# Two modulation tiles at a visit, a longer stretch for them, and another order of the first loads

## The chip, the cores and the metric

One core of a Trainium2 chip runs the kernel. The metric is the time on the device in microseconds; the median of three runs is given. TensorE multiplies matrices (PE; its weight loads, PEld, overlap with it), VectorE is DVE, ScalarE is ACT, GpSimd is POOL, and SyncE (SP) issues nearly all transfers.

## What is computed

Two transformer blocks in a row on x (256 tokens by 1024), in fp32. The first block has a layer with differential attention beside an HGRN2 recurrence, and a layer with dilated attention, each with a feed-forward part and a gated embedding. The second block has two layers that mix gated linear attention, neighborhood attention and sliding-window attention, and it also carries a context of 256 tokens. Its norms are scaled, shifted and gated by modulations, which depend only on two small vectors `c` and `c_ctx`:

```python
s_lat = jax.nn.silu(c)
s_ctx = jax.nn.silu(c_ctx)
xc = ctx
for i in range(DEPTH):                       # DEPTH = 2
    mod = (s_lat @ w_mod[i] + b_mod[i])[:, None, :]
    mod_c = s_ctx @ w_mod[i] + b_mod[i]
    ...
    h = rms_norm_2(x, norm_mix[i]) * (1.0 + sc1) + sh1
    hc = rms_norm_2(xc, norm_mix[i]) * (1.0 + sc1c) + sh1c
    y, yc = token_mixers(h, hc, ...)
    x = x + g1 * y
```

## The kernel before

**Weights as a stream.** All weights stand in one array of tiles of 128 x 1024 fp32 (512 KB, eight blocks of 128 x 128). There are 410 tiles for the main path (x), read through a ring of 5 buffers (`ring`), and 96 modulation tiles (`w_mod`), read through `ring_mod` of 4 buffers. The context ("side" stream) reads 110 of the main path's later tiles a second time, through a ring of 2 (`ring_side`). For main and side tiles ScalarE makes a high part (`high`, L533) and VectorE the rest (`low`, L541), and each product of a block with 256 tokens is three matmuls, L566, L567 and L568 (L605 to L607 where tokens are stationary). So one such tile is 24 matmuls. x is split in the same way (L639, L647) before the first product.

**Modulations.** A modulation tile isn't split. Its products take two vectors at once: four matmuls (L695) on 32 columns of the array each, eight records of the profile. Eight tiles make a pass, after which ScalarE copies the rows (L723), TensorE turns them with `c_ident` (L707), and VectorE adds the bias (L737). There are 12 passes. `MOD_PLAN` spreads the tiles evenly over the first 250 us of the planner's clock. They depend on nothing in the first block, and the first block doesn't need them. The context's part depends on the last pass: `tensor_contexts` waits for it, and the loads of `ring_side` wait for the last tile to be used. `SIDE_PLAN` gives the pace of the context's tiles.

**The order of work** is made when the kernel is built. Each engine is a lane with a clock in microseconds, and each piece of work is a generator that says what it waits for (`yield name`) and how long it takes (`tick`). The planner takes the piece that can begin first; among those that can begin by then it takes the one of lowest rank, and of equal rank the one that was added first. A `Pace` has a low rank (first) while it is behind its plan, and a high one (only when nothing else is ready) when it is not. The result is a fixed order on every engine; a wrong guess of the planner becomes a wait on the chip, with all that is behind it on that engine. SP is such a lane too: `sync_loads`, `sync_tiles` and `sync_mod_tiles` are its pieces, and it issues in a fixed order.

**Start.** SP issues the two halves of x, the parameters (`par`), 11 constants, the context (`Xc`, 1 MB), five ring tiles and four modulation tiles, in this order. Parameters and constants count on one semaphore, `s_start`; whoever needs the parameters waits for the last constant. A load's time is planned as 0.1 us of SP, 1.3 us of distance to the next of the same piece, and 3.3 us to landing.

Of the kernel before, what the change touches and what calls it, by code (L numbers as in the profile page):

```python
# [103 lines left out]
TB = 8  # L104
RING, SPLIT = 5, 3
RING_SIDE, SPLIT_SIDE = 2, 2
RING_MOD = 4
MAIN_TILES, MOD_TILES = 410, 96
# [5 lines left out]
GLOBAL_CONSTS = ["ident", "meanD", "mean128", "mean64", "before", "after", "cols"]  # L114
ROPE_CONSTS = ["cos1", "sin1", "rot1"]
# [130 lines left out]
def T_us(n, passes=1):  # L246
    return max(n * passes / 2270.0, 0.06) + 0.006


def A_us(n):  # L250
    return 0.2 + n / 1200.0


def V_us(n):
    return 0.15 + n / 960.0
# [6 lines left out]
class Program:  # L262
    def __init__(self, nc, ctx, io):
# [19 lines left out]
        self.s_pool = signal("gpsimd_steps")  # L283
        self.s_raw_mod = [signal(f"mod_tile_loaded{i}") for i in range(RING_MOD)]
        self.s_xload = [signal(f"x_loaded{i}") for i in range(2)]
        self.s_start, self.s_ctx = signal("constants_loaded"), signal("ctx_loaded")
        self.s_consts, self.s_bias = signal("stage_constants_loaded"), [signal(f"bias_loaded{i}") for i in range(2)]
        self.s_p, self.s_wa2, self.s_out = signal("p_loaded"), signal("wa2_loaded"), signal("stored")

        self.main = Stream(self, "main", RING, SPLIT, None)  # L290
        self.side = Stream(self, "side", RING_SIDE, SPLIT_SIDE, second_tiles("c", 0) + second_tiles("c", 1))
        self.s_tile, self.s_low, self.split = [], self.main.s_low.sem, 0
        self.mod_blocks, self.blocks, self.loaded = [], [], None
        x, c = self.px, self.pc = Path("x", 1), Path("c", 0)
        x.stream, c.stream = self.main, self.side

# [15 lines left out]
        for w in (x, c):  # L312
# [11 lines left out]
            n = 512 if w is x else SEQ  # L324
# [152 lines left out]

def sync_loads(k):
    nc, io, D_, x = k.nc, k.io, k.D, k.px
    for i, half in enumerate((slice(0, DC // 2), slice(DC // 2, DC))):  # L480
        nc.sync.dma_start(x.X[:, half, :], io["x"][:, half]).then_inc(
            *D_.tick(k.s_xload[i], 0.1, ("x loaded", i), by=16, later=5.0))
    k.add(D_, sync_tiles(k, k.main), 0)
    yield None
    for buffer, name in [(k.par, "params")] + [(k.c[n], n) for n in GLOBAL_CONSTS + ROPE_CONSTS + ["causal"]]:
        nc.sync.dma_start(buffer[:, :], io[name]).then_inc(
            *D_.tick(k.s_start, 0.1, ("loaded", name), by=16, later=4.0))
        yield None
    k.marks["constants"] = D_.last
    k.add(D_, sync_mod_tiles(k), 1)  # L490
    nc.sync.dma_start(k.pc.X[:, :, :], io["ctx"]).then_inc(
        *D_.tick(k.s_ctx, 0.1, ("ctx loaded",), by=16, later=9.0))
    k.add(D_, sync_tiles(k, k.side), 1)


def sync_tiles(k, st):

    nc, D_ = k.nc, k.D
    n = MAIN_TILES if st.plan is None else len(st.plan)
    if st is k.side:  # L500

        D_.wait_for((yield "mod used", MOD_TILES - 1))
    for j in range(n):
        if j >= st.n_ring:
            D_.wait_for((yield st.name, "used", j - st.n_ring))
        else:
            yield None
        at = j if st.plan is None else TILE_AT[st.plan[j]]
        nc.sync.dma_start(st.ring[:, j % st.n_ring, :], k.io["stream"][at]).then_inc(
            *D_.tick(st.s_raw[j % st.n_ring], 0.1, (st.name, "raw", j), by=16, later=3.3))  # L510
        D_.clock += 1.3


def sync_mod_tiles(k):

    nc, D_ = k.nc, k.D
    for j in range(MOD_TILES):
        if j >= RING_MOD:
            D_.wait_for((yield "mod used", j - RING_MOD))
        else:  # L520
            yield None
        nc.sync.dma_start(k.ring_mod[:, j % RING_MOD, :], k.io["stream"][MAIN_TILES + j]).then_inc(
            *D_.tick(k.s_raw_mod[j % RING_MOD], 0.1, ("mod raw", j), by=16, later=3.3))
        D_.clock += 1.3


def scalar_high(k, st):
# [125 lines left out]
def vector_setup(k):  # L653
    nc, V = k.nc, k.V
    nc.vector.memset(k.zeros[:, :], 0.0).then_inc(*V.tick(k.s_vec, V_us(SEQ)))
    nc.vector.memset(k.keep[:, :], 1.0).then_inc(*V.tick(k.s_vec, V_us(SEQ)))
    V.wait_ge(k.s_vec, V.last)
    nc.vector.memset(k.keep[:, :].rearrange("p (c t) -> p c t", t=CH)[:, :, 0:1], 0.0).then_inc(
        *V.tick(k.s_vec, 0.15, ("keep",)))
    nc.vector.memset(k.cs[:, :, :], 0.0).then_inc(*V.tick(k.s_vec_bg, V_us(256), ("cs", "zero")))  # L660
    V.wait_ge(k.s_start, (yield "constants"))
    nc.vector.tensor_scalar(k.negsink, k.col("sink", 0, 12), -1.0, None, ALU.mult).then_inc(
        *V.tick(k.s_vec, 0.15, ("negsink",)))


def scalar_setup(k):
    nc, A = k.nc, k.A
    A.wait_ge(k.s_start, (yield "constants"))
    cc = k.col("cc", 0, 16)
    A.wait_ge(k.s_vec_bg, (yield "cs", "zero"))  # L670
    k.tables("silu")
    nc.scalar.activation(k.cs[:, :, 0:2], cc.rearrange("p (c s) -> p c s", s=2), ACT.Silu).then_inc(
        *A.tick(k.s_act_bg, 1.5, ("cs",)))
# [8 lines left out]
def tensor_modulations(k):  # L682
    nc, T = k.nc, k.T
    T.wait_ge(k.s_act_bg, (yield "cs",))
    for layer in range(DEPTH):
        for i in range(MOD_PASSES):
            b = yield from k.pc.gemm.take(T, ("row", layer, i))
            k.bank_of["rows", layer, i] = b
            for c in range(DC):
                tile = len(k.mod_blocks) // TB  # L690
                k.mod_blocks += [("w_mod_2", layer, c, 8 * i + j) for j in range(8)]
                raw = k.ring_mod[:, tile % RING_MOD, :]
                T.wait_ge(k.s_raw_mod[tile % RING_MOD], (yield "mod raw", tile))
                for j in range(4):
                    m = nc.tensor.matmul(k.bank[b][32 * j:32 * j + 32, 0:256], k.cs[:, c, :],  # L695
                                         raw[:, 256 * j:256 * j + 256], start=(c == 0), stop=(c == DC - 1),
                                         skip_group_check=True)
                if c == DC - 1:
                    m.then_inc(*T.tick(k.s_mod_rows, MOD_US, ("rows", layer, i), ("mod used", tile)))
                else:  # L700
                    m.then_inc(*T.tick(k.s_used_mod, MOD_US, ("mod used", tile)))
                yield None
            T.wait_ge(k.s_act_bg, (yield "row", layer, i))
            b = yield from k.pc.gemm.take(T, ("mod", layer, i))
            k.bank_of["mod turned", layer, i] = b
            for j in range(2):
                m = nc.tensor.transpose(k.bank[b][:, j * P:(j + 1) * P], k.rows[:, j * P:(j + 1) * P],  # L707
                                        k.c["ident"][:, :])
            m.then_inc(*T.tick(k.s_mod_turned, 2 * T_us(256), ("mod turned", layer, i)))
            yield None  # L710


MOD_US = 0.5


def scalar_modulations(k):
# [24 lines left out]
def rstd(k, mean, out, eps, read, key):  # L741

    nc, A = k.nc, k.A
    n = out.shape[1]
    k.tables("ln")
    nc.scalar.activation(out, mean, ACT.Ln, bias=k.c["cols"][:, eps:eps + 1]).then_inc(
        *A.tick(k.s_rstd, A_us(n), read))
    A.wait_ge(k.s_rstd, A.last)
    k.tables("exp")
    nc.scalar.activation(out, out, ACT.Exp, scale=-0.5).then_inc(*A.tick(k.s_rstd, A_us(n), key))  # L750
    yield None
# [398 lines left out]
def tensor_squares(k, w, tag):  # L1150
    nc, T, n = k.nc, k.T, SEQ
    yield tag, "square", 0
    b = yield from w.banks.take(T, (tag, "log"))
    k.bank_of[tag, "squares"] = b
    for i in range(DC):
        T.wait_ge(k.s_squares, (yield tag, "square", i))
        nc.tensor.matmul(k.bank[b][:, 0:n], k.c["meanD"][:, :], w.SQ[:, k.sq_of[tag, i], 0:n], start=(i == 0),
                         stop=(i == DC - 1)).then_inc(*T.tick(k.s_sums, T_us(n, 4), (tag, "summed", i)))
        yield None
# [274 lines left out]
def vector_lambda(k):  # L1434
    nc, V = k.nc, k.V
    c = k.px.small[:, 48:56]
    lp = k.col("lam", 0, 256)
    V.wait_ge(k.s_start, (yield "constants"))
    for i in range(2):
        a, b = lp[:, 128 * i:128 * i + 64], lp[:, 128 * i + 64:128 * i + 128]  # L1440
        nc.vector.tensor_tensor_reduce(a, a, b, 1.0, 0.0, ALU.mult, ALU.add, c[:, i:i + 1]).then_inc(
# [906 lines left out]
def load_stream(k, tiles):  # L2348
    assert tiles >= MAIN_TILES + MOD_TILES
    k.add(k.D, sync_loads(k), 0)  # L2350
# [26 lines left out]
        return self.late if self.done() < due else self.rank  # L2377


MOD_PLAN = [(0, 0), (250, MOD_TILES)]  # L2380
SIDE_PLAN = [(250, 0), (820, 35), (1400, 110)]


def emit(k):
# [3 lines left out]
    k.add(T, tensor_products(k, x), 1)  # L2388
    mods = Pace(k, lambda: len(k.mod_blocks) / TB, MOD_PLAN, -3, 3)
    side = Pace(k, lambda: len(k.side.blocks) / TB, SIDE_PLAN, -6, 5)  # L2390
    k.add(T, tensor_modulations(k), mods)
# [5 lines left out]
    k.add(A, x_high(k), 0)  # L2397
    k.add(V, x_low(k), 0)
    k.add(V, vector_setup(k), 1)
    k.add(A, scalar_setup(k), mods)  # L2400
    k.add(A, scalar_modulations(k), mods)
    k.add(V, vector_modulations(k), mods)
# [318 lines left out]
```

## Time and profile before

| | |
|---|---|
| runs | 1936.05, 1930.65, 1936.8 us (median 1936.05) |
| the profiled execution's own time | 1936.03 us |
| its span | 1934.7 us |
| mean granted clock of TensorE | 0.979 of full speed |
| busy | PE 1830.1 us (95%), DVE 1268.5 (66%), ACT 1000.2 (52%) |
| HBM read | 331.55 MB, 172 GB/s over the span |

All positions in time are microseconds from the span's start. Rows of matmuls show the modelled duration, which overlaps with the next one; the distance from start to start is what a matmul costs. "Idle before" is the time in which the engine had nothing under way, with what ended it.

### The profile page before, as it was taken

How to read it: one execution, taken by the hardware profiler on the slowest of the kernel's cores; microseconds unless marked ns; L12 is line 12 of the kernel's file. 1: busy time of each engine (PE TensorE's matmuls, PEld its weight loads, DVE VectorE, ACT ScalarE, POOL GpSimd, SP SyncE). 2: the span in 40 equal slices, each digit the busy share in tenths (PEclk: the TensorE clock that was granted, in tenths of full speed). 3: DMA queues.
4: the chain of work that ended last, by engine and by line, in shares of the span. 5: the costliest groups of instructions: out<-in, count | busy, mean ns of one | idle time of the engine just before them, and what ended most of it. 6: DMA issues, size and time to landing. Idle time of an engine off the chain costs nothing. (4 is left out here: it accounts for less than half of the span.)

```text
span 1934.7 us, 35649 instructions
## 1 busy us (share of the span) xinstructions
PE 1830.1 (95%) x14792; PEld 1675.2 (87%) x14792; DVE 1268.5 (66%) x2327; ACT 1000.2 (52%) x1748; POOL 77.5 (4%) x78
## 2 busy tenths in 40 slices
PE   5998899999999989999988999999999989889997
PEld 3775699998888969999988998899999978589997
DVE  3535565667867786666666677776775667756665
ACT  3444443547755565454465565554554455544443
POOL 0000100002000020000020010100100000100000
PEclk9999999999999999999998999999999989989999
DMA  8898875563454425555544444355555533235553
GB/s 320 296 314 296 266 235 188 181 202 113 138 171 131 141 66 166 190 182 190 184 131 156 152 153 132 110 164 185 179 172 172 176 120 110 66 104 181 185 185 120
DMA packets 93824, 334.91 MB, mean 173 GB/s; under 512 B 10960, under 2 KB 12880, under 8 KB 93536
## 3 DMA queue, kind: packets, MB, share of 16 engines
q1 hardware_dynamic: 92016, 327.33, 51.6%
q0 software_dynamic: 1648, 5.31, 0.9%
q8 instruction: 117, 1.92, 0.4%
q14 instruction: 43, 0.35, 0.1%
HBM read 331.55 MB, written 1.05 MB: 172 GB/s over the span
## 5 line engine op out<-in xcount | busy, mean ns | idle before, releaser
L541 DVE TENSOR_TENSOR low<-ring,high 128x1024 fp32r<-128x1024 f32 x410 | 501.5, 1224 | 260.4 <-ACT high L533 257.6
L566 PE MATMUL bank<-XHx,high 128*128 128x256 f32 x2096 | 613.1, 293 | 36.3 <-DVE XLx L647 20.9
L533 ACT CAST high<-ring 128x1024 fp32r<-128x1024 f32 x410 | 428.6, 1045 | 329.9 <-PE bank L568 277.4
L567 PE MATMUL bank<-XLx,high 128*128 128x256 f32 x2096 | 594.9, 284 | 0.0
L568 PE MATMUL bank<-XHx,low 128*128 128x256 f32 x2096 | 594.6, 284 | 0.0
L566 PEld LDWEIGHTS bank<-XHx,high 128*128 128x128 f32 x2096 | 401.8, 192 | 67.5 <-issue 47.1
L567 PEld LDWEIGHTS bank<-XLx,high 128*128 128x128 f32 x2096 | 403.0, 192 | 1.0
L568 PEld LDWEIGHTS bank<-XHx,low 128*128 128x128 f32 x2096 | 403.1, 192 | 0.0
L566 PE MATMUL bank<-XHc,high_side 128*128 128x256 f32 x608 | 181.7, 299 | 13.3 <-DVE low_side L541 11.7
L567 PE MATMUL bank<-XLc,high_side 128*128 128x256 f32 x608 | 172.8, 284 | 0.0
L568 PE MATMUL bank<-XHc,low_side 128*128 128x256 f32 x608 | 172.4, 284 | 0.0
L541 DVE TENSOR_TENSOR low_side<-ring_side,high_side 128x1024 fp32r<-128x1024 f32 x110 | 136.6, 1243 | 51.8 <-ACT high_side L533 49.7
L533 ACT CAST high_side<-ring_side 128x1024 fp32r<-128x1024 f32 x110 | 115.2, 1047 | 73.9 <-DMA ring_side<-in_stream 73.5
L566 PE MATMUL bank<-hidden_high,high 128*128 128x256 f32 x512 | 143.5, 280 | 0.0
L568 PE MATMUL bank<-hidden_high,low 128*128 128x256 f32 x512 | 143.4, 280 | 0.0
L567 PE MATMUL bank<-hidden_low,high 128*128 128x256 f32 x512 | 142.6, 279 | 0.0
L566 PEld LDWEIGHTS bank<-XHc,high_side 128*128 128x128 f32 x608 | 116.7, 192 | 24.4 <-issue 15.5
L567 PEld LDWEIGHTS bank<-XLc,high_side 128*128 128x128 f32 x608 | 116.9, 192 | 0.3
L568 PEld LDWEIGHTS bank<-XHc,low_side 128*128 128x128 f32 x608 | 117.1, 193 | 0.0
L566 PE MATMUL bank<-x_hidden_high,high 128*128 128x256 f32 x352 | 99.4, 282 | 1.8 <-DVE x_hidden_low L1281 1.8
L567 PE MATMUL bank<-x_hidden_low,high 128*128 128x256 f32 x352 | 98.4, 279 | 0.0
L568 PE MATMUL bank<-x_hidden_high,low 128*128 128x256 f32 x352 | 98.1, 279 | 0.0
(448 smaller groups left out, 3078.9 us busy)
## 6 DMA issues: line engine op xcount, KB each, us to landing
ring<-in_stream SPq DMA_DIRECT2D x410, 512.0 KB, 3.6
ring_side<-in_stream SPq DMA_DIRECT2D x110, 512.0 KB, 3.7
ring_mod<-in_stream SPq DMA_DIRECT2D x96, 512.0 KB, 5.4
x_nb<-in_rpb POOLq DMA_DIRECT2D x6, 256.0 KB, 3.3
x_late_NB<-in_rpb POOLq DMA_DIRECT2D x6, 256.0 KB, 3.2
Xx<-in_x SPq DMA_DIRECT2D x2, 512.0 KB, 4.6
Xc<-in_ctx SPq DMA_DIRECT2D x1, 1024.0 KB, 6.5
out<-y SPq DMA_DIRECT2D x8, 128.0 KB, 2.0
```

The lines of the kernel that those rows point to most:

```text
L533: nc.scalar.copy(st.high[:, j % st.n_split, :], st.ring[:, j % st.n_ring, :]).then_inc(*A.tick(st.s_high, A_us(TB * P), (st.name, "high", j)))
L541: nc.vector.tensor_tensor(st.low[:, j % st.n_ring, :], st.ring[:, j % st.n_ring, :], st.high[:, j % st.n_split, :].bitcast(F32), ALU.subtr ...
L566: nc.tensor.matmul(out, wh, xh, start=(i == 0), stop=False)
L567: nc.tensor.matmul(out, wh, xl, start=False, stop=False)
L568: m = nc.tensor.matmul(out, wl, xh, start=False, stop=(c == ks[-1]))
```

## The change

- `sync_loads` issues half of x, a ring tile, the parameters, the other half of x and a second ring tile; then the constants, then the context. The tiles' piece and the modulations' piece are added before the constants, at ranks 0 and 1, but behind `sync_loads` in the lane.
- The parameters get a semaphore of their own (`s_par`). `negsink`, the lambda and the silu of `c` wait for it alone. The turns of the modulations, the root of the norms and the sums of squares wait for the constants instead.
- A load's planned time: 0.45 us of SP, and `landing` keeps one account for all loads that use it: each takes 1.5 us behind the one before, and 2.0 us on top.
- `tensor_modulations` takes two tiles at a visit (`MOD_BATCH`), without a step between them, and both must have landed in the plan. The planned time of a tile is 0.43 us, and 0.45 us for the visit.
- `MOD_PLAN` ends at 480 rather than 250. `SIDE_PLAN` begins at 480 rather than 250 and has 35 tiles at 850 rather than 820; its end stays.

```diff
 def sync_loads(k):
     nc, io, D_, x = k.nc, k.io, k.D, k.px
+    tiles = sync_tiles(k, k.main)
+    next(tiles)
     for i, half in enumerate((slice(0, DC // 2), slice(DC // 2, DC))):
+
         nc.sync.dma_start(x.X[:, half, :], io["x"][:, half]).then_inc(
-            *D_.tick(k.s_xload[i], 0.1, ("x loaded", i), by=16, later=5.0))
-    k.add(D_, sync_tiles(k, k.main), 0)
+            *D_.tick(k.s_xload[i], 0.45, ("x loaded", i), by=16, later=landing(k, D_)))
+        next(tiles)
+        if i == 0:
+            nc.sync.dma_start(k.par[:, :], io["params"]).then_inc(
+                *D_.tick(k.s_par, 0.45, ("params",), by=16, later=landing(k, D_)))
+    k.add(D_, tiles, 0)
+    k.add(D_, sync_mod_tiles(k), 1)
     yield None
-    for buffer, name in [(k.par, "params")] + [(k.c[n], n) for n in GLOBAL_CONSTS + ROPE_CONSTS + ["causal"]]:
-        nc.sync.dma_start(buffer[:, :], io[name]).then_inc(
-            *D_.tick(k.s_start, 0.1, ("loaded", name), by=16, later=4.0))
+    names = GLOBAL_CONSTS + ROPE_CONSTS + ["causal"]
+    for name in names:
+        nc.sync.dma_start(k.c[name][:, :], io[name]).then_inc(*D_.tick(k.s_start, 0.45, by=16, later=4.0))
         yield None
+
+    for name in names:
+        k.marks["loaded", name] = D_.last
     k.marks["constants"] = D_.last
-    k.add(D_, sync_mod_tiles(k), 1)
...
+def landing(k, lane):
+
+    k.loads = max(k.loads, lane.clock) + 1.5
+    return k.loads - lane.clock + 2.0
...
         nc.sync.dma_start(st.ring[:, j % st.n_ring, :], k.io["stream"][at]).then_inc(
-            *D_.tick(st.s_raw[j % st.n_ring], 0.1, (st.name, "raw", j), by=16, later=3.3))
-        D_.clock += 1.3
+            *D_.tick(st.s_raw[j % st.n_ring], 0.45, (st.name, "raw", j), by=16, later=landing(k, D_)))
...
         for i in range(MOD_PASSES):
+            first = len(k.mod_blocks) // TB
+            yield "mod raw", first + MOD_BATCH - 1
             b = yield from k.pc.gemm.take(T, ("row", layer, i))
             k.bank_of["rows", layer, i] = b
             for c in range(DC):
                 tile = len(k.mod_blocks) // TB
+                if c % MOD_BATCH == 0:
+
+                    yield "mod raw", tile + MOD_BATCH - 1
                 k.mod_blocks += [("w_mod_2", layer, c, 8 * i + j) for j in range(8)]
                 raw = k.ring_mod[:, tile % RING_MOD, :]
-                T.wait_ge(k.s_raw_mod[tile % RING_MOD], (yield "mod raw", tile))
+                T.wait_ge(k.s_raw_mod[tile % RING_MOD], k.marks["mod raw", tile])
...
-                yield None
+                if c % MOD_BATCH == 0:
+                    T.spend(0.45)
+            yield None
             T.wait_ge(k.s_act_bg, (yield "row", layer, i))
             b = yield from k.pc.gemm.take(T, ("mod", layer, i))
             k.bank_of["mod turned", layer, i] = b
+            T.wait_ge(k.s_start, (yield "constants"))
...
-MOD_US = 0.5
+MOD_US, MOD_BATCH = 0.43, 2
...
-MOD_PLAN = [(0, 0), (250, MOD_TILES)]
-SIDE_PLAN = [(250, 0), (820, 35), (1400, 110)]
+MOD_PLAN = [(0, 0), (480, MOD_TILES)]
+SIDE_PLAN = [(480, 0), (850, 35), (1400, 110)]
```

## Rows read from the trace of the kernel before

**Rows 1.** Busy time by stretch: length, busy (instructions) PE PEld DVE ACT POOL, clock, DMA.

```profile
21.00:140.00 119.00, 117.94 (x987) 88.65 (x988) 54.67 (x130) 52.54 (x106) 0.00 (x0) 1.00 0.88 304
140.00:245.00 105.00, 92.90 (x779) 62.61 (x777) 59.52 (x114) 47.30 (x81) 9.55 (x10) 0.93 0.84 285
245.00:420.00 175.00, 175.00 (x1486) 171.15 (x1484) 104.78 (x144) 81.23 (x124) 0.53 (x1) 1.00 0.61 197
420.00:480.00 60.00, 53.76 (x394) 49.08 (x393) 46.15 (x85) 42.17 (x81) 10.26 (x8) 0.91 0.43 143
```

**Rows 2.** Groups up to 500 us: busy us, mean ns, idle before, its releaser.

```profile
L695 PE MATMUL bank<-ring_mod,TMPc 128*32 128x256 f32 x768 | 61.7, 409 | 9.1 <-DMA ring_mod<-in_stream 9.1
```

**Rows 3.** The start in order of time: start us, us, engine, line, operation.

```profile
0.74 0.86 SPq L481 DMA_DIRECT2D Xx<-in_x  x2
...
8.35 3.04 SPq L509 DMA_DIRECT2D ring<-in_stream  x5
...
15.68 1.04 ACT L533 CAST high<-ring 128x1024 fp32r<-128x1024 f32 x1 [13.66 <-DMA ring<-in_stream]
...
16.76 1.23 DVE L541 TENSOR_TENSOR low<-ring,high 128x1024 fp32r<-128x1024 f32 x1 [4.14 <-ACT high L533]
...
20.93 0.55 PE L566 MATMUL bank<-XHx,high 128*128 128x256 f32 x1 [20.93 <-DVE XLx L647]
...
21.28 0.41 PE L567 MATMUL bank<-XLx,high 128*128 128x256 f32 x1
...
21.49 0.41 PE L568 MATMUL bank<-XHx,low 128*128 128x256 f32 x1
```

**Rows 4.** Transfers, 0 to 21 us in 40 slices, and issues with us to landing.

```profile
GB/s 0 0 0 148 304 289 195 265 406 390 318 397 356 321 313 291 248 294 355 417 449 328 437 375 359 437 414 414 437 398 429 421 406 429 414 414 437 398 390 445
...
ring<-in_stream SPq DMA_DIRECT2D x5, 512.0 KB, 8.9
...
Xx<-in_x SPq DMA_DIRECT2D x2, 512.0 KB, 4.6
```

**Rows 5.** Timeline of TensorE around a visit of one tile and of two.

```profile
65.39 0.28 PE L567 MATMUL bank<-XLx,high 128*128 128x256 f32 x1
65.51 0.28 PE L568 MATMUL bank<-XHx,low 128*128 128x256 f32 x1
65.72 0.64 PE L695 MATMUL bank<-ring_mod,TMPc 128*32 128x256 f32 x8
66.29 0.38 PE L566 MATMUL bank<-XHx,high 128*128 128x256 f32 x1
...
243.03 1.07 PE L695 MATMUL bank<-ring_mod,TMPc 128*32 128x256 f32 x16
244.03 0.39 PE L566 MATMUL bank<-XHx,high 128*128 128x256 f32 x1
```

**Rows 6.** Timeline of TensorE from the last modulation tile to the context's first product.

```profile
428.01 0.64 PE L695 MATMUL bank<-ring_mod,TMPc 128*32 128x256 f32 x8
...
435.27 1.22 PE L1157 MATMUL bank<-SQx,c_meanD 128*128 128x256 f32 x2 [2.96 <-ACT SQx L1167]
...
438.22 0.41 PE L567 MATMUL bank<-p_low,high 128*128 128x256 f32 x1
...
442.05 0.47 PE L566 MATMUL bank<-XHc,high_side 128*128 128x256 f32 x1
```

**Rows 7.** Modulation matmuls alone, by stretch: PE busy (x), PEld busy (x), clock, DMA.

```profile
21.00:140.00 119.00, 28.58 (x360) 7.44 (x360) 1.00 0.88 304
140.00:245.00 105.00, 27.98 (x344) 8.38 (x344) 0.93 0.84 285
245.00:420.00 175.00, 4.47 (x56) 1.10 (x56) 1.00 0.61 197
```

**Rows 8.** Waits of TensorE from 140 to 245 us: us, times, longest.

```profile
PE bank L695 <- DMA ring_mod<-in_stream: 8.1, 6, 2.2
```

**Rows 9.** Instructions with the context's high parts: PE, PEld, DVE, ACT busy.

```profile
420.00:480.00 60.00, 21.12 (x102) 16.84 (x103) 8.55 (x7) 7.78 (x8) 0.91 0.43 143
```

More of the change, by code:

```diff
@@ L285, in __init__ @@
         self.s_xload = [signal(f"x_loaded{i}") for i in range(2)]
-        self.s_start, self.s_ctx = signal("constants_loaded"), signal("ctx_loaded")
+        self.s_par, self.s_start, self.s_ctx = signal("params_loaded"), signal("constants_loaded"), signal("ctx_loaded")
         self.s_consts, self.s_bias = signal("stage_constants_loaded"), [signal(f"bias_loaded{i}") for i in range(2)]
@@ L292, in __init__ @@
         self.s_tile, self.s_low, self.split = [], self.main.s_low.sem, 0
-        self.mod_blocks, self.blocks, self.loaded = [], [], None
+        self.mod_blocks, self.blocks, self.loaded, self.loads = [], [], None, 0.0
         x, c = self.px, self.pc = Path("x", 1), Path("c", 0)
@@ L522, in sync_mod_tiles @@
         nc.sync.dma_start(k.ring_mod[:, j % RING_MOD, :], k.io["stream"][MAIN_TILES + j]).then_inc(
-            *D_.tick(k.s_raw_mod[j % RING_MOD], 0.1, ("mod raw", j), by=16, later=3.3))
-        D_.clock += 1.3
+            *D_.tick(k.s_raw_mod[j % RING_MOD], 0.45, ("mod raw", j), by=16, later=landing(k, D_)))
 def scalar_high(k, st):
@@ L660, in vector_setup @@
     nc.vector.memset(k.cs[:, :, :], 0.0).then_inc(*V.tick(k.s_vec_bg, V_us(256), ("cs", "zero")))
-    V.wait_ge(k.s_start, (yield "constants"))
+    V.wait_ge(k.s_par, (yield "params",))
     nc.vector.tensor_scalar(k.negsink, k.col("sink", 0, 12), -1.0, None, ALU.mult).then_inc(
@@ L667, in scalar_setup @@
     nc, A = k.nc, k.A
-    A.wait_ge(k.s_start, (yield "constants"))
+    A.wait_ge(k.s_par, (yield "params",))
     cc = k.col("cc", 0, 16)
@@ L744, in rstd @@
     n = out.shape[1]
+    A.wait_ge(k.s_start, (yield "constants"))
     k.tables("ln")
@@ L1152, in tensor_squares @@
     yield tag, "square", 0
+    T.wait_ge(k.s_start, (yield "constants"))
     b = yield from w.banks.take(T, (tag, "log"))
@@ L1437, in vector_lambda @@
     lp = k.col("lam", 0, 256)
-    V.wait_ge(k.s_start, (yield "constants"))
+    V.wait_ge(k.s_par, (yield "params",))
     for i in range(2):
```

## The prediction

> **What bounds the kernel now.** I first read the stretches [rows 1]: for each stretch they give how long TensorE was busy, its granted clock and the DMA share. From 21 to 140 us TensorE is busy 117.94 of 119 us, and from 245 to 420 us all of 175. There every microsecond of TensorE work is a microsecond of the kernel. It is idle before 21 us, for 12.1 us in 140 to 245 and for 6.2 in 420 to 480. In these two later stretches the granted clock falls under 1.00 (0.93, 0.91), so part of the work runs at 1.2 GHz. The rest of the span holds no edit, only work that is ordered anew. So the time is TensorE's work, plus its idle time, plus what the lower clock costs, and the sum below is made of changes in these three.
>
> Then I read the groups of instructions up to 500 us [rows 2]: before modulation matmuls TensorE stands idle for 9.1 us, all of it until a tile has landed. Next the start in order of time [rows 3]: x is issued at 0.74 us, then parameters, eleven constants and the context, and the first ring tile only from 8.35. Its cast starts at 15.68, and the first matmul at 20.93. [Rows 4] say how long transfers took and at what rate.
>
> **First loads.** After the change SP issues half of x, tile 0, the parameters, the other half of x and tile 1, and only then the eleven constants, the context and the other tiles: the constants are a planner part that comes before the ring's tiles at each step, so tile 2 still stands behind all of them. Tile 0 takes the place of the second half of x, issued near 1.2 us; with the 4.6 us of x [rows 4] it lands near 6, its high part takes 1.04 and its low part 1.23 us [rows 3], and with the splitting of x the first matmul comes near 8.5. Tile 1 ends the first 2.6 MB (two halves of x, two tiles, parameters, and 0.26 MB that GpSimd loads), which the slices of [rows 4], 0.525 us each, give by about 10 us, so it is landed by 11 and ready by 13.3. Tile 2 has the same bytes ahead of it as today and lands when it does today, issued near 9.3 and landed 8.9 us later [rows 4]: 18.2, ready at 20.5. A tile is 24 matmuls; at full clock they start 0.12 us apart [rows 5], so 2.85 us, and at the low clock 0.21 us apart [rows 3], so 5 us. Tile 0 ends near 13.5, tile 1 near 16.3, and TensorE then waits 4.2 us for tile 2. The start therefore gives two tiles, 5.7 us, and 0.4 us from 20.93 to 20.5: 6.1 us, not the 12.4 by which the first matmul is earlier. Bounds: 4 (tile 1 late too) and 9.
>
> The low clock enters here. After an idle time of 2.96 us at 432 to 435 [rows 6] the matmuls that follow take 0.41 us as those of the start do [rows 3], not the 0.28 of the full clock, so I count the restart at 20.5 as cold as today's start and take nothing for the clock. The Trainium skill, "TensorE: Matmul & The Clock Gate", section "HAM oscillation", warns of just this, short work followed by a wait for a load, and this speaks against starting early: by that rule the early tiles run cold and the restart too, which is what I counted. Without the restart being cold it would give about 2 us more.
>
> The Trainium skill, "DMA: Bandwidth & Descriptors", section "Specifications", names about 358 GB/s from HBM for a core; the slices from 12 us on in [rows 4] show 359 to 445, most of them over 400. By the page's figure the 1.6 MB of context and tile 2 would take 0.6 us longer than at 0.41 MB/us; the measurement decides.
>
> **Two tiles at a visit.** A single visit today [rows 5]: the last matmul before starts at 65.51, the visit at 65.72, the next product at 66.29; without it the next would start 0.12 later, so a visit costs 0.66 us. A double one without a stall starts at 243.03 and the next product at 244.03: 0.21 + 1.00 - 0.12 = 1.09 us. Pairing saves 0.23 us. Today's 96 tiles (768 records in [rows 2], eight a tile) are taken in 76 visits, counted as runs of this matmul with no other between, of which [rows 5] show two; after the change in 48: 28 x 0.23 = 6.4 us. Bounds 4 (a visit merged in an idle stretch is worth nothing) and 6.4.
>
> **Over twice the stretch.** By records [rows 7] hold 45 tiles in 21 to 140 us, 43 in 140 to 245, 7 in 245 to 420; the last one comes at 428.01 [rows 6]. The plan falls from 96/250 to 96/480 = 0.2 tiles per us, so about 24 tiles fall before the main path's first idle stretch. The others are not removed: they fill the idle places from there on, 16 or so are forced between the feed-forward products, and some 15 to 20 are left for the idle place after them. By itself this only moves work. What it can win is stalls: of the 9.1 us, 8.1 lie in 140 to 245, in six waits of up to 2.2 us [rows 8], in bursts for which the planner believes in a load each 1.4 us. The new `landing` says 1.5 us per load on one account for all streams and lets a visit wait for both tiles, so visits are put later. But the ring holds four tiles still, only two visits, and the main chain there (its scan, exponentials and LayerNorm) has waits of its own. I take 5 us, bounds 0 and 9.1. Queued behind such a wait are the products of that chain, on the same engine; that is why any of it counts.
>
> **Contexts later.** The context's loads wait until the last modulation tile is used. That one ran at 428.01 today, the context's first product followed at 442.05 [rows 6], and 21.12 us of context products (high part; in all 102 x 1.5 / 24 = 6.4 tiles, 18 us of issue) filled 420 to 480 [rows 9]. Afterwards 15 to 20 modulation tiles (0.55 us each, 8 to 11 us) fill this place first, and the context comes some 25 us later. These 18 us of context work are then forced in where TensorE is full, while the 8 to 11 us of modulations have left the full places: the idle time is what differs, 7 to 10 us, less what the main path gains because ScalarE and VectorE (46 of 60 us busy) do not split context tiles there. I take a loss of 4; bounds: a gain of 6.2 (all idle time there goes [rows 1]) and a loss of 21.1.
>
> The waits on the parameters alone (negsink, lambda, silu) and the new waits on constants cost nothing: the last of today's constants lands before 12.0 us, two tiles more ahead of them add under 3 us, and the first matmul that reads one comes after 30; if they were late, tile products behind it would wait.
>
> **Sum.** The profiled execution took 1936.03 us, span 1934.7, and the median of the three runs is 1936.05. 1936 - 6.1 - 6.4 - 5 + 4 = 1922.5 us.
>
> **Rivals.**
> - *Starved start, stalls stay.* Tile 1 late as well, everything cold: 1936 - 2 - 6.4 - 0 + 4 = 1931.6. For it: DMA share 0.9 over the whole start; against it: tile 1 has only 2.4 MB before its end.
> - *More than summed.* The stalls go (9.1) and the idle time of 420 to 480 too (6.2): 1936 - 6.1 - 6.4 - 9.1 - 6.2 = 1908.2. For it: VectorE is freed there. Against: today's context work is what fills it.
> - *Slower: the filler is missing.* Where the 21.1 us of context products stood, TensorE stands idle, and its clock falls as in this stretch today: 1936 - 6.1 - 6.4 - 5 + 21.1 = 1939.6. It decides once the idle time in this stretch grows by over 17.5 us. For it: little but modulations is ready there, at 0.55 us of work per 512 KB against 2.85; against: 15 tiles are left over, and the main path's own LayerNorm and gate take the engines.
> - *The pace does nothing* (modulations run ahead in idle places just as before) and only order changes: within 0.3%.
>
> **Chances.** Forecast 0.50, own range 1914 to 1930. More than summed 0.18, starved start 0.15, slower 0.13, nothing 0.04. The bound of 0.3% is 5.8 us, about what a measurement of this kernel can tell from no change: faster means under 1930.2. The forecast, the larger gain and a part of the starved start give faster 0.71; same 0.15; slower 0.14. For 8 in 10 the range takes in the starved start and most of the large gain: 1905 to 1936.
>
> **What the profile after would show.** First matmul near 8.5 us, then a wait of 4 us before the third tile; L695's rows sixteen at a time; waits for ring_mod under 5 us; PE full up to an earlier first idle stretch, some 20 us sooner; about 15 modulation tiles after the feed-forward part, and the first context product after 440 us of today's count; idle time there about 10 us. I am wrong if that idle time reaches 20 us, if tile 2 comes earlier than 15 us, or if new stalls stand behind 480 us, where every order of work is planned anew.

## The result and the profile after

The changed kernel takes 1897.3 us (median of 4 runs, 1895.24 to 1903.14) against 1935.53 for the kernel before (4 runs): a ratio of 0.9813, 95% interval 0.9801 to 0.9826, so 38.2 us faster. The forecast was 1922.5, a gain of 13.5, and the range ended at 1905. The direction is right and the size is not. The profiled execution is the slowest of its four: 1903.14 us, span 1901.8.

The stretches of [rows 1] after the change, in the same columns (length, busy and instructions of PE, PEld, DVE, ACT, POOL, then granted clock, DMA share, GB/s), then the rest of the span:

```profile
21.00:140.00 119.00, 117.31 (x916) 94.48 (x917) 67.83 (x146) 67.70 (x131) 0.00 (x0) 0.96 0.77 267
140.00:245.00 105.00, 96.20 (x844) 79.93 (x843) 64.16 (x117) 45.37 (x81) 10.09 (x10) 0.95 0.75 250
245.00:420.00 175.00, 173.18 (x1528) 161.29 (x1526) 99.62 (x142) 79.25 (x125) 2.89 (x3) 1.00 0.75 239
420.00:480.00 60.00, 58.86 (x428) 51.81 (x425) 48.95 (x86) 39.13 (x64) 7.02 (x7) 1.00 0.71 236
480.00:1480.00 1000.00, 974.37 (x7958) 918.73 (x7957) 703.08 (x1329) 554.40 (x991) 48.79 (x43) 1.00 0.50 156
```

The idle time of 420 to 480 fell from 6.2 us to 1.1 and the clock there rose from 0.91 to 1.00; in 140 to 245 idle fell from 12.1 to 8.8. From 21 to 140 us the clock is 0.96 where it was 1.00. The transfers are spread: their share fell before 245 us and rose after. The modulation matmuls alone, same stretches (PE, PEld):

```profile
21.00:140.00 119.00, 17.77 (x256) 6.94 (x256) 0.96 0.77 267
140.00:245.00 105.00, 17.07 (x224) 5.78 (x224) 0.95 0.75 250
245.00:420.00 175.00, 15.23 (x224) 5.64 (x224) 1.00 0.75 239
420.00:480.00 60.00, 4.25 (x68) 1.77 (x64) 1.00 0.71 236
```

That is 32, 28, 28 and 8 tiles where [rows 7] had 45, 43 and 7. Waits of TensorE up to 500 us (us, times, longest):

```profile
PE bank L580 <- DVE low L555: 10.9, 2, 9.0
PE bank L714 <- DMA ring_mod<-in_stream: 6.6, 9, 1.5
PE bank L1181 <- ACT SQx L1191: 3.4, 2, 2.8
PE bank L580 <- DVE XLx L661: 2.4, 1, 2.4
```

The start in order of time (start, duration, engine, line), against [rows 3]:

```profile
0.74 0.39 SPq L484 DMA_DIRECT2D Xx<-in_x  x1
...
1.18 0.42 SPq L525 DMA_DIRECT2D ring<-in_stream  x1
...
2.12 0.63 SPq L484 DMA_DIRECT2D Xx<-in_x  x1
...
2.79 0.56 SPq L525 DMA_DIRECT2D ring<-in_stream  x1
...
9.01 0.55 PE L580 MATMUL bank<-XHx,high 128*128 128x256 f32 x1 [9.01 <-DVE low L555]
...
9.58 1.66 SPq L525 DMA_DIRECT2D ring<-in_stream  x3
...
14.20 1.23 DVE L555 TENSOR_TENSOR low<-ring,high 128x1024 fp32r<-128x1024 f32 x1 [3.49 <-DMA c_causal<-in_causal]
...
15.48 0.41 PE L580 MATMUL bank<-XHx,high 128*128 128x256 f32 x1 [1.93 <-DVE low L555]
...
18.00 1.04 ACT L547 CAST high<-ring 128x1024 fp32r<-128x1024 f32 x1 [5.33 <-DMA ring<-in_stream]
...
18.95 0.70 ACT L653 CAST XHx<-Xx 128x256 fp32r<-128x256 f32 x2
...
20.69 0.58 PE L580 MATMUL bank<-XHx,high 128*128 128x256 f32 x1 [2.45 <-DVE XLx L661]
```

The first product is at 9.01 instead of 20.93. But TensorE then stops twice. The stop that ends at 15.48 is a wait for the second tile's low part. Its high part was done at 12.36, but VectorE made the low part only at 14.20, when the last constant (`c_causal`) had landed. The kernel gives the reason: the first statement of `vector_attention` is a wait for the constants, and the planner put it in VectorE's order just ahead of this low part. The kernel before has the same statement; there VectorE had nothing else to do at that time. The stop that ends at 20.69 is not a wait for the third tile: it is for the last two parts of x, which ScalarE cast at 18.95, behind the cast of the third tile, which had waited 5.33 us for its load.

In the waits above, 9.0 of the 10.9 us for `low` are the start and 1.9 the stop at 15.48.

Two views of a visit and of the end of the modulations, against [rows 5] and [rows 6]:

```profile
314.26 0.28 PE L582 MATMUL bank<-XHx,low 128*128 128x256 f32 x1
314.47 1.07 PE L714 MATMUL bank<-ring_mod,TMPc 128*32 128x256 f32 x16
315.47 0.39 PE L580 MATMUL bank<-XHx,high 128*128 128x256 f32 x1
...
447.25 1.93 PE L714 MATMUL bank<-ring_mod,TMPc 128*32 128x256 f32 x32
...
472.03 0.28 PE L580 MATMUL bank<-XHc,high_side 128*128 128x256 f32 x1
```

**Where the time went.** All orders run the same products, so I laid every TensorE start-to-start distance to one of these (us, from one trace each; products' own time is equal and left out; "low clock" is the excess over the full-clock distance):

| | before | after | plans alone (e1) |
|---|---|---|---|
| first product | 20.9 | 9.0 | 21.7 |
| modulation visits, with their waits | 77.6 | 65.2 | 74.5 |
| other small gaps, under 0.45 each | 149.1 | 143.0 | 143.9 |
| idle, from main tile 0 to 35 | 0.0 | 8.1 | 0.5 |
| idle, tiles 92 to 110 | 6.4 | 0.7 | 0.7 |
| idle, all other | 60.5 | 58.5 | 51.8 |
| low clock | 19.2 | 16.3 | 13.1 |
| sum of these | 333.7 | 300.8 | 306.2 |

Tiles 92 to 110 are the stretch between the first block's dense feed-forward products and the following layer's: 415.8 us onwards before, 389.3 to 471.8 after. The row of visits takes in every wait just before or after modulation matmuls, also those in tiles 92 to 110: the idle time there by the profile's own rows is 3.0 us in the changed kernel and 4.7 in e1, not 0.7. A profile is one execution, and one kernel's runs lie up to 16 us apart, partly with the clock. So I also use the mean over all runs of the span times (1 minus the granted clock), called *clock loss* below: it bounds what a full clock would give, and it is more than the clock costs, since TensorE is also idle or held by others in some of that time (in the profile before it is 40.6 us, and the table has 19.2). Before it is 35 us in each comparison (mean span about 1933, clock 0.982); after, 27.5 (1896.9, 0.9855). So at most some 7 of the 38 us are clock.

### The profile page after: what moved, and what is told of

It reads as the page before. It is cut to its first block and busy times, and to the rows that moved or that the text cites. A ratio compares the mean times of both kernels' runs of the same rounds, so it can differ in the third digit from the quotient of the medians.

```text
span 1901.8 us, 35689 instructions
## 1 busy us (share of the span) xinstructions
PE 1812.8 (95%) x14792; PEld 1673.5 (88%) x14792; DVE 1267.8 (67%) x2327; ACT 995.9 (52%) x1744; POOL 79.2 (4%) x78
## 5 line engine op out<-in xcount | busy, mean ns | idle before, releaser
L580 PE MATMUL bank<-XHx,high 128*128 128x256 f32 x2096 | 612.0, 292 | 21.2 <-DVE low L555 10.9
L580 PE MATMUL bank<-XHc,high_side 128*128 128x256 f32 x608 | 177.7, 292 | 7.8 <-DVE low_side L555 7.7
L580 PEld LDWEIGHTS bank<-hidden_high,high 128*128 128x128 f32 x512 | 96.2, 188 | 2.4 <-issue 2.4
```

The lines of the kernel that those rows point to most:

```text
L580: nc.tensor.matmul(out, wh, xh, start=(i == 0), stop=False)
```

## The experiments

All ratios are to the kernel before, run beside it, with 95% intervals. Because the planner finds no order for some paces, a few kernels use the nearest one that it finds; the diffs show them.

**e1 to e4: one part alone, or all but one.** e1 is the kernel before with only the paces:

```diff
-MOD_PLAN = [(0, 0), (250, MOD_TILES)]
-SIDE_PLAN = [(250, 0), (820, 35), (1400, 110)]
+MOD_PLAN = [(0, 0), (480, MOD_TILES)]
+SIDE_PLAN = [(480, 0), (840, 35), (1400, 110)]
```

> The kernel before with the two paces alone: modulations over 480 us, contexts from 480 (35 tiles at 840, since with 850 the planner finds no order for this kernel). Theory A (the paces carry the gain behind 420 us: context work leaves the stretch where the main path is held by ScalarE and VectorE, and lands in places that were idle): 12 to 20 us faster, about 1920, with idle time in 420 to 480 no larger than before and less idle in 640 to 1060. Theory B (the new load times of the planner carry it): within 4 us of before. Theory C (any new order moves the time by some us without a cause in the edit): anything between -8 and +8, with the gain spread over stages.

e2 is the kernel before with only the planned times of loads: 0.45 us of SP each, and `later=landing(k, D_)` for x and the tiles.

> The kernel before with the planner's new load times alone (0.45 us of SP, one account of 1.5 us a load, 2.0 us on top); order of the first loads, visits and paces as before. Theory A: the waits of modulation matmuls for their tiles fall from 9.1 to under 5 us, the rest stays: 2 to 6 us faster. Theory B: 12 us faster or more, with less idle time all over the span.

e3 is the kernel before with only the new order of the first loads and the semaphore `s_par`, planned by the old times.

> The kernel before with the order of the first loads and the separate semaphore of the parameters alone. Theory A: first matmul near 9 us, then waits; worth 3 to 6 us, since tile 2 and the late parts of x hold the products until about 20.7. Rival: the whole 11.9 us by which the first matmul is earlier.

e4 is the changed kernel with the old `MOD_PLAN` and `SIDE_PLAN`.

> The changed kernel with the two old paces (modulations over 250 us, contexts from 250 with 35 tiles at 820). Theory A: it loses the 12 to 20 us of the paces and keeps start, pairs and fewer stalls: 1912 to 1920. Theory B: it stays within 4 us of the changed kernel, 1897 to 1901.

| kernel | median us | ratio | clock loss us |
|---|---|---|---|
| e1 paces alone | 1908.14 | 0.9856 (0.9817 to 0.9895) | 23.8 |
| e2 load times alone | 1928.24 | 0.9963 (0.9945 to 0.9982) | 35.5 |
| e3 first loads alone | 1933.47 | 0.9984 (0.9962 to 1.0006) | 35.7 |
| e4 all but the paces | 1917.55 | 0.9917 (0.9885 to 0.9949) | 38.7 |

The paces, which I had booked as a loss of 4, gain 26 us alone and some 20 on top of the rest. The load times gain 7, but not in the way that I expected: TensorE's wait for modulation tiles stays at 8.9 us in e2, where it was 9.1. Where these 7 us come from isn't shown. The first loads alone give 3, inside their interval.

**e5 and e6: is it the place where the contexts begin?** The first theory was that the context's products, moved behind the norm and gate, stop being in the main path's way there. e5 holds the last modulation tile back until main tile 105 is used, with the modulations' pace as before:

```diff
+                if tile == MOD_TILES - 1:
+                    yield "main", "used", 105
...
-SIDE_PLAN = [(250, 0), (820, 35), (1400, 110)]
+SIDE_PLAN = [(440, 0), (845, 35), (1400, 110)]
```

> The kernel before, 95 modulation tiles as today; only the last one is held in the order until main tile 105 is used (in the changed kernel it comes there), so that the context's products begin there too, at a pace from 440 us with 35 tiles at 845. Theory A (it is the place at which the context begins, away from the norm and the gate between the two layers, that gives most of the 26 us of the two paces): 12 to 20 us faster than before. Rival D (it is the modulations spread over 480 us, which leave the first stretches and fill the later idle places): within 4 us of before, or slower, as TensorE has nothing to fill 430 to 470 with.

e6 changes the context's pace alone, to `[(480, 0), (835, 35), (1400, 110)]`.

> The kernel before with the contexts' pace alone (from 480 us, 35 tiles at 835): context products may still fill places near 440 us in which nothing else is ready, but are not forced. Theory A: less than half of the gain of the held tile, 0 to 8 us faster, since they still begin in the norm's stretch. Rival E (it is the forced context tiles that cost): 12 us faster or more.

Measured: e5 1935.52 us, 1.0004 (0.9987 to 1.0021); e6 1934.59 us, 0.9995 (0.9977 to 1.0013). In e5 the first context product moved from 442 to 489 us and won nothing. So the place alone isn't the cause.

**e7: the modulations' pace alone** (`MOD_PLAN` 480, the rest as before).

> The kernel before with the modulations' pace alone (480 us); contexts keep their plan (from 250, 35 tiles at 820), but can't begin before the last modulation tile. Theory A: the context begins late anyway and then is forced to catch up with its plan; most of the gain stays, 12 to 24 us faster. Rival E: little gain, since the tiles are forced in.

Measured: 1923.5 us, 0.9935 (0.9911 to 0.9959), clock loss 30.4: 12 of the 26 us.

**e9, e13, e14: other lengths of the pace** in the changed kernel: 380, 430 and 500 instead of 480. e12 is the changed kernel again, in the same comparison as e9.

> The changed kernel with the modulations' pace ending at 380 us rather than 480; contexts still from 480. The last modulation tiles then come before the norm between the two layers of the first block (near 400 us), and nothing is left to fill it: contexts are not due. Theory F (what the two paces win is that modulation tiles, cheap and free of ScalarE and VectorE, fill that norm's stretch, where before them context tiles or nothing did): idle and low clock there come back, 6 to 12 us slower than the changed kernel, 1903 to 1910. Rival G (only that modulations leave the first 140 us counts): under 3 us slower.

> The changed kernel once more, to stand beside these on the same chip: 1895 to 1900 us. Its profile should show the first matmul at 9.0 us again, the second start at 15.5, the third at 20.7; the low clock may lie differently from execution to execution.

> The changed kernel with the modulations spread over 430 us of the planner's clock instead of 480 (380 gave 1910.1, 480 gives 1899.2 and 1897.3). Theory of the filler (modulation tiles left for the stretch between the feed-forward part and the next layer's products replace idle time and low clock there): fewer tiles are left over than the 22 of 480 and more than the none of 380, so the time lies between, near 1903, and the idle time of that stretch between 0.7 and 6 us. Rival (380 was a bad order by chance, the pace itself is indifferent): as the changed kernel, within 3 us of 1898.

> The changed kernel with 500 instead of 480. Theory of the filler: the stretch is filled already with 22 tiles, idle only 0.7 us, so more tiles win nothing there: 1896 to 1902, the stretch up to the context's first product grows by the few tiles moved into it and the one before shrinks alike. A loss, over 1904, would show that the context, which waits for the last tile, becomes late.

| pace | median us | ratio | modulation tiles after main tile 92 | idle + low clock, tiles 92 to 110, without waits at visits | clock loss |
|---|---|---|---|---|---|
| 380 (e9) | 1910.11 | 0.9876 (0.9855 to 0.9897) | 0 | 8.6 | 35.9 |
| 430 (e13) | 1923.09 | 0.9935 (0.9911 to 0.9958) | 10 | 10.4 | 46.9 |
| 480 (e12) | 1899.19 | 0.9823 (0.9797 to 0.9849) | 20 | 0.7 | 28.1 |
| 500 (e14) | 1902.5 | 0.9833 (0.9809 to 0.9857) | 24 | 0.0 | 29.5 |

The windows of tiles 92 to 110, of e9, then of e13, then of the changed kernel:

```profile
395.00:480.20 85.20, 79.55 (x521) 72.64 (x520) 65.71 (x114) 55.88 (x100) 10.03 (x9) 0.96 0.48 151
```

```profile
395.70:482.70 87.00, 81.30 (x559) 70.94 (x558) 63.49 (x110) 51.93 (x92) 11.58 (x9) 0.94 0.59 188
```

```profile
389.30:471.80 82.50, 79.54 (x620) 66.50 (x619) 61.98 (x108) 52.15 (x92) 9.91 (x9) 1.00 0.79 264
```

The changed kernel does 99 more matmuls than e9 (160 of its 620 are modulations) in 2.7 us less. TensorE is idle in it for 3.0 us, against 5.7 in each of the others, and it has full clock where e9 and e13 have 0.96 and 0.94. Waits of e9's TensorE there show how (idle before it in brackets); the matmul after the longest takes 0.55 us, not 0.39:

```profile
411.49 0.39 PE L580 MATMUL bank<-p_high,high 128*128 128x256 f32 x1 [0.75 <-ACT e L1342]
...
413.39 1.17 PE L1181 MATMUL bank<-SQx,c_meanD 128*128 128x256 f32 x4 [0.92 <-ACT SQx L1191]
...
425.53 0.55 PE L580 MATMUL bank<-XHx,high 128*128 128x256 f32 x1 [3.36 <-DVE XLx L1219]
```

So in this stretch the tiles left over do act as filler, and it is no slope: 10 are used up before the waits come (the last one at main tile 97, at 418.1 us; the first wait over 0.9 us ends at 423.5) and save nothing; 20 reach to tile 106 and save about half of the idle time and all of the low clock. That is some 5 of the 11 us by which e9 is slower than e12; the rest lies in other stages. The time of the whole kernel follows the filler less well: my expectation for 430, a time between, missed by 20 us, and 430 is 11 to 13 us slower than 380, which has no filler at all. Of e13's 22 us over e12 in mean span, up to 19 are clock loss, and by the two traces the low clock cost it more than e12 in six of eight stages (30.7 us against 15.2 in all). Why this order is put at the low clock so often isn't settled.

**e8, e10, e15, e16: the start.** e8 puts two more ring tiles, four in all, ahead of the constants (two more `next(tiles)` before they are issued). e10 puts the first loads back in their old order in the changed kernel.

> The changed kernel with ring tiles 2 and 3 issued before the constants and the context (the planner believes in landings near 9 and 11 us; in truth tile 2 now lands near 13 rather than 17). Theory A (tile 2 behind 2 MB of constants and context, and the last two parts of x cast after it, hold the products until 20.7 us): the wait before 20.69 shrinks from 7 us to 2, the clock falls less; 3 to 6 us faster than the changed kernel, about 1892. Rival: no gain, as the tiles behind them and the modulations come later instead.

> The changed kernel with x, parameters, constants and context ahead of all ring tiles again (separate semaphore kept). By the comparison of the first 105 us in the traces the new order gives 11.9 us at the first matmul and loses 4.7 to waits and 3.5 to the low clock: 3 to 5 us slower than the changed kernel, about 1901. Rival: the 6.1 us of the forecast, or nothing, as the single edit to the kernel before showed 1 to 3 us.

e15 is the changed kernel with the context's pace at 860, the control for e16, which has the constants and the context on the account of loads as well:

```diff
     for name in names:
+        k.loads = max(k.loads, D_.clock) + 0.3
...
+    k.loads = max(k.loads, D_.clock) + 3.0
     nc.sync.dma_start(k.pc.X[:, :, :], io["ctx"]).then_inc(
```

> The changed kernel with the context's first 35 tiles at 860 instead of 850: the control for the next run, and a measure of what a new order of the second block is worth by itself. Both theories: within 5 us of the changed kernel, 1893 to 1904.

> The run before (context's pace 860) with the constants and the context on the planner's account of loads too (0.3 us a constant, 3 us the context), so that the planner knows that the third tile lands near 18 us, not 11.5. Theory of the start (the last parts of x are cast behind the third tile's cast, which waits for its load, so TensorE stops after some 12 products): the casts of x now come before that cast, two whole tiles of products run before 20 us, the idle time before 21 us falls from 4.7 to under 3 us, and the first main tiles come 1 to 2 us sooner; the whole 0 to 4 us faster than the run before. Rival (VectorE's wait for the last constant and the load of the third tile set the restart anyway): the third tile starts no sooner than 20.5 and nothing is won, within 2 us of the run before.

| kernel | median us | ratio | clock loss |
|---|---|---|---|
| e8 tiles before constants | 1897.25 | 0.9796 (0.977 to 0.9823) | 27.5 |
| e10 old first loads | 1911.65 | 0.9877 (0.9849 to 0.9905) | 34.0 |
| e15 control | 1899.43 | 0.9821 (0.9801 to 0.9841) | 30.8 |
| e16 all loads on the account | 1901.67 | 0.9833 (0.9814 to 0.9853) | 29.5 |

The start of e16:

```profile
9.40 0.55 PE L582 MATMUL bank<-XHx,high 128*128 128x256 f32 x1 [9.40 <-DVE low L557]
...
11.64 1.01 ACT L655 CAST XHx<-Xx 128x256 fp32r<-128x256 f32 x3
...
15.44 0.39 PE L582 MATMUL bank<-XHx,high 128*128 128x256 f32 x1 [0.60 <-DVE low L557]
...
15.91 0.28 PE L582 MATMUL bank<-XHx,high 128*128 128x256 f32 x1
...
22.96 0.39 PE L582 MATMUL bank<-XHx,high 128*128 128x256 f32 x1 [0.25 <-DVE low L557]
```

The last parts of x are cast at 11.64, all 48 matmuls of two tiles are done before the third starts at 22.96, and there is no stop like that of 2.45 us. The third tile's products start at 26.3 in e15, 3.3 us later. So the cause of the second stop is shown.

The first stop is not mended by this. The second tile starts at 15.44 in e16, at 15.09 in e15 and at 15.48 in the changed kernel, each time behind VectorE's wait for the last constant (e15, then e16):

```profile
13.81 1.23 DVE L555 TENSOR_TENSOR low<-ring,high 128x1024 fp32r<-128x1024 f32 x1 [3.38 <-DMA c_causal<-in_causal]
```

```profile
14.16 1.23 DVE L557 TENSOR_TENSOR low<-ring,high 128x1024 fp32r<-128x1024 f32 x1 [3.77 <-DMA c_causal<-in_causal]
```

TensorE's idle time there is only 0.60 us in e16 because the first tile's matmuls run at the low distance of 0.21 us to their end at 14.8, where those of the changed kernel are at full clock from 12.33 and end at 13.5. In e8 the same wait stands one tile later, since its constants land last:

```profile
11.93 1.23 DVE L557 TENSOR_TENSOR low<-ring,high 128x1024 fp32r<-128x1024 f32 x1 [1.50 <-ACT high L549]
...
16.38 1.23 DVE L557 TENSOR_TENSOR low<-ring,high 128x1024 fp32r<-128x1024 f32 x1 [2.88 <-DMA c_causal<-in_causal]
...
17.99 0.39 PE L582 MATMUL bank<-XHx,high 128*128 128x256 f32 x1 [2.73 <-DVE XLx L663]
```

There the second tile follows without a stop, and TensorE stops once, for 2.73 us, behind that wait. No run moves the wait alone, so its price isn't measured. In time e8 missed its expectation of about 1892 by 5 us.

e16 isn't faster: by main tile 20 the two are level (105.0 and 104.8), for e16 has then visited two modulation tiles more, and the rest is another order. e10 missed its expectation of about 1901: it says that the first loads are worth 12 us by medians and 11 by mean spans in the changed kernel (against e12), not 3. Up to 6 of these are clock loss (34.0 against 28.1), and its profiled execution, at 0.985 the fastest of its six, is only 4.6 above e12's 1896.3. What the rest is, I can't name.

**e11: two tiles at a visit alone** (in the kernel before, context's pace at 810).

> The kernel before with two tiles at a visit and their planned times alone (contexts' 35 tiles at 810 rather than 820, since with 820 the planner finds no order). 76 visits become 46 or so, 0.23 us each: 6.9 us by the rows of a visit; stalls as they were: 4 to 8 us faster, about 1928. Rival: longer waits for two tiles at once cost as much again, no change.

Measured: 1926.35 us, 0.9961 (0.9946 to 0.9975): 7 us.

## Why the prediction was right or wrong

- **First loads, 6.1 us: right mechanism, two waits missed.** The first product came at 9.01 (said: near 8.5) and the third tile landed at 18.0 (said: 18.2). I had two whole tiles done by then; by 20.69 there were 36 matmuls of 48. The second tile came late because VectorE stood at the constants until 14.20: My sentence that waits cost nothing spoke of the parameters and of the new waits on constants, and looked only at matmuls that read one; this wait is an old one, of VectorE, and isn't in it. And the last casts of x stood behind the third tile's. By the trace the start gives 11.9 earlier, less 4.7 idle and 3.5 low clock up to tile 20: 3.7 us. Alone it measured 3, with an interval that holds 0; taken back in the changed kernel it cost 11 to 12 (e10). The restart was cold as counted: the matmuls from 20.69 take 0.41 us, and the warning of the Trainium skill, "TensorE: Matmul & The Clock Gate", section "HAM oscillation", held in this trace. In e16 with a gap of 0.60 the next ones took 0.28, and in e15 after a gap of 1.63 too.
- **Two tiles at a visit, 6.4 us: right.** A visit takes 0.21 + 1.00 - 0.12 = 1.09 us by the rows at 314.26 to 315.47, as read before. There are 44 visits, not 48 (a few hold four tiles): 32 fewer by 0.23 is 7.4 us, and e11 measured 7.
- **Stalls, 5 us: half of it, and not by the cause I gave.** The wait for modulation tiles fell from 9.1 [rows 2] to 6.6, so 2.5 us, and my own sign, under 5, wasn't met. Visits with their waits cost 77.6 and 65.2 us: 12.4, of which 7.4 are the visits; the remaining 5.0 hold other waits too. I had expected the gain from the longer stretch and from `landing`. Neither lowers this wait alone: it is 12.0 us in 17 waits in e1 and 8.9 in e2.
- **"Contexts later", a loss of 4, bounds -6.2 and +21.1: the step that failed**, with the sentence before it, that the longer stretch "by itself only moves work". The two paces gain 26 us alone (e1) and some 20 in the changed kernel (e4). The other three terms, 17.5 us together, agree with the 17 that e4 measured, so the whole miss is this term: with a gain of 20 in its place the sum gives 1898.5. That the three agree so well is partly luck, since first loads alone gave 3 and the load times 7 that aren't the stalls. I had the left-over tiles nearly right (15 to 20; there are 20), but valued them as an exchange for context work. They are a better filler: the stretch's idle time and low clock went from 9.9 us to 0.7, and without them (e5, e6: 13.0 and 11.7 us; e9: 8.6) they stayed. Waits at the visits come on top of the 0.7. By its row TensorE is idle there in e1 for 4.7 us, at full clock:

```profile
391.80:479.30 87.50, 82.79 (x645) 66.85 (x643) 61.94 (x108) 52.67 (x92) 9.89 (x9) 1.00 0.81 267
```

So this stretch accounts for 5 of the 26 us in e1, and for 7 of the whole in the changed kernel (3.0 left).
- **The part that my sum had no term for.** In e1 a further 5.5 us of idle and low clock go in tiles 110 to 140, a stage where I had written "no edit, only work that is ordered anew". With the modulations' pace alone (e7) the context begins as late but must make up for it by its old pace, and this stage gets worse instead (10.3 to 13.6); with the context's pace alone there is no filler. That may be why 12 and 0 make 26 together; it is read from one trace each, and which wait went isn't shown by an experiment. A second part is the clock in tiles 20 to 35 (before, then e1):

```profile
130.10:248.70 118.60, 106.50 (x898) 73.57 (x897) 65.87 (x123) 54.32 (x91) 10.08 (x10) 0.94 0.85 287
```

```profile
112.90:220.60 107.70, 97.98 (x860) 70.72 (x857) 65.61 (x121) 53.15 (x90) 10.20 (x10) 1.00 0.83 291
```

It is 0.94 in the changed kernel's profile too (105.3 to 217.0) and 1.00 in e12's, which is the same kernel, so one trace can't credit it to the paces. The rest of the 26 us is not located.
- **The clock.** I took nothing for it. Clock loss, a bound, fell by 12 us in e1, by about 11 from e4 to the changed kernel, and by 7 over the whole change.
- **The rivals.** "More than summed" (0.18) was the nearest: it named the idle time of 420 to 480, and most of that went (6.2 to 1.1). Its time was 1908.2, still 11 us too slow. "The filler is missing" named the right danger, but the tiles of the pace were that filler; e9 and e13 are what its absence looks like, still faster than before.
- **The parts add up roughly.** e1 26, e2 7, e3 3 and e11 7 are 43; together they gave 38.

No kernel here is measurably faster than the changed one (e8 is 2 us ahead of e12, within the intervals).

## What to carry to other kernels

Work that depends on nothing is worth most where TensorE would otherwise wait, so count the idle time of the later stretches before you say that spreading it "only moves work", and see that it lasts until the waits are over; half a reserve (e13) gave nothing here. Two paces of which one waits for the other should be changed together and tested together: alone these gave 12 and 0, both 26. When first loads are reordered, look at every engine that stands in line behind a load that still comes late: here ScalarE's casts of x behind the third tile, and VectorE behind the last constant. Putting the loads on the planner's account (e16) removed the stop behind ScalarE's casts, though it didn't make the kernel faster.

## What the runs showed of the hardware that was not expected

The granted clock goes with part of the spread of one kernel's runs. The six of e10 go from a span of 1900.9 us at 0.985 to 1914.8 at 0.980, without any change in the program. The tie isn't close in every kernel: e11 has a run of 1922.4 us at 0.979 and one of 1927.7 at 0.983. The mean clock also differs between orders of the same work: 0.9875 for e1, 0.9756 for e13. So one profile can't price an order to better than some 10 us here, and the mean clock of all runs belongs beside the median.
